# Last products of each row tile half by half of the width, and retention's output projection begun ahead of the last head's turn

## The chip, the cores and the metric

The kernel runs on one core of one Trainium2 chip. TensorE multiplies, VectorE and ScalarE split the weights and do the elementwise work, GpSimd does powers of small columns, SyncE issues the weight loads. The metric is the device time of one launch in microseconds; the kernel before has a median of 3464.42 us over three runs (3463.05 to 3464.59).

## The reference

Two blocks run one behind the other on 256 rows of width 1024, all in float32. Cut to what matters here:

```
# first block, two layers
for l in range(2):
    x = x + 0.5 * swiglu(rms_norm(x, g), w_gate_up, w_down)          # f10, f11
    u = rms_norm(x, mix_norm) @ w_in
    y = concat([ssd_mixer(u), mlstm_mixer(u), rwkv7_mixer(u)])       # m0, m1
    x = x + y @ w_out                                                # out0, out1
    x = x + 0.5 * swiglu(rms_norm(x, g), w_gate_up, w_down)          # f20, f21
x = rms_norm(x, final_norm)
# second block, two layers, x beside a context of 256 rows until the second mixer
half_ffn(t, m, j) = t + 0.5 * m[3j+2] * swiglu_2(modulate(rmsnorm(t), m[3j], m[3j+1]))
layer 0: x, ctx = half_ffn(.,0)  [half00]; += m[5] * fourier_layer  [four]; half_ffn(.,2)  [half02]
layer 1: x, ctx = half_ffn(.,0)  [half10]; x += m[5] * retention    [ret, retout]; x = half_ffn(x,2)  [half12]
return rmsnorm(x, final_g)
# retention, per head: two-sided decayed attention y; then
out = (silu(g) * (y - mean) * rsqrt(var + eps)) @ ret_w_out          # 2048 x 1024
```

## The kernel before, in words

Every large product is done in three passes on split numbers: a float32 matrix is written as a high and a low part, and `mm3` (L103, each product at L100) issues high by high, high by low and low by high into one PSUM bank. A weight tile is [128, 2048] elements (1 MB). SyncE loads it into one of up to eight `raw` places; ScalarE writes its high part into one of two or three `hi` buffers (`split_hi`, L305); VectorE writes the low part over the raw place (`split_lo`, L311). Half-width or single-chunk tiles have 1024 columns.

The program is a list of stages, each a set of generators, one for each engine, that are stepped together: `run(stage)` in `network` appends one phase of a stage to an order, and every engine issues its own instructions of each phase in that order. `Core.plan` attaches the weight tiles to phases and puts each `split_hi`/`split_lo` at the earliest phase at which its `hi` buffer is free and no more than the allowed number of tiles is ahead. Each instruction counts up a semaphore; other engines wait on the count (`mark`, `wait_ge`). Each engine executes in order.

A stage's output projection: the K rows of the product come in chunks of 128, two chunks to a weight tile. The result rows come in tiles `t` of 128 (two for 256 rows, four with the context), the 1024 columns in two halves `h` of 512, and each (t, h) has its own PSUM bank. For all groups of tiles but the last the order is chunk, then row tile, then half. The last group (two weight tiles together, in Fourier one) goes row tile by row tile: for each `t` all its chunks, and inside each chunk both halves. When the last product of (t, h) is done, its bank is marked `back`, and VectorE drains it into the residual: `Half` (L717) and `Whole` (L2438) in one operation, `Gated` in two (L699 multiplies by the gate, L701 adds). The next stage's `Norm` squares each half row on ScalarE as it is finished, takes the power on GpSimd, scales (L588 on VectorE, ScalarE beside it), and TensorE transposes the normed rows (L546) for the next products. `join` interleaves the last phases of a stage with the first of the norm.

High buffers (`his`): 3 for the feed-forward stages of 256 rows (f10, f20, f11, f21, half12), 2 for those of 512 rows (half00, half02, half10), for the mixers' projections (`MixOut`: out0, out1) and for retention's (`Out`). The feed-forward stages have 22 chunks (the 512-row ones in two parts of 11, whose last tile holds a single chunk); `MixOut` and `Out` have 16 chunks, tiles 0 to 7, and the last group is tiles 6 and 7.

Retention (`Ret`) has 26 phases: for each of four heads the projections of q, k, v and gate, the scores, the product with v, silu of the gate (ScalarE, L2826), the normed and gated `y` (VectorE, L2876), eight transposes of it (L2787, the "turn") into banks 4 and 5, and two copies into `yT` (ScalarE, L2831). Then `Out` waits for all of `Ret` (`enter`), splits `yT` in four quarters into `ys` high (L2407) and low (L2416), and runs its products into banks 4 to 7. `ys` lies over the normed rows that `Ret` reads. The gate vector of the residual is made by the `Gates` stage in bank 3, four transposing products at a time (L100 on `retdg`), stepped between the first phases of `Out`.

Of the kernel before, what the change touches and what calls it, by code (L numbers as in the profile page):

```python
# [729 lines left out]
class Ffn(Stage):  # L730
# [44 lines left out]
    def tensor(self, p):  # L775
# [3 lines left out]
        for k, count in enumerate(self.parts):  # L779
            K.ada_bank = 3 if nt == 2 else 7 - 4 * (k % 2)  # L780
            K.ada_bank_free = self.dv["out", k - 1, 3, 1] if k else None
            for j in range(count):
                wh, wl = (w.rearrange("p (k h n) -> p k h n", k=8, h=2) for w in self.ready(p, n))
                if nt == 2 and J >= 3:
                    p.wait_ge(*self.dv["mul", J - 3])
                if nt == 4 and j >= 2:
                    p.wait_ge(*self.dv["mul", J - 2])
                elif nt == 4 and k:
                    p.wait_ge(*self.dv["out", k - 1, j, 1])
                for h, o in enumerate(self.pair(k, J)):  # L790
                    for c in range(8):
                        if J == 0:
                            self.norm.ready(p, c)
                        x = mm3(p, o, wh[:, c, h, :], wl[:, c, h, :], hs[0][:, c, 0:N], hs[1][:, c, 0:N], c == 0, c == 7)
                x.then_inc(*p.mark(self.pe, "tile", n))
                n, J = n + 1, J + 1
                yield
            if nt == 4:
                K.ada.clear(p)
            if self.finish.gates:  # L800
                self.finish.gates.done(p)
            if nt == 4 and k:
                p.wait_ge(*self.dv["out", k - 1, 3, 1])
            for group in self.groups[k]:
                parts = [(i, c) for i in group for c in range(min(2, count - 2 * i))]
                ends = group == self.groups[k][-1]
                if ends:
                    order = [(a, t) for t in range(nt) for a in parts]
                else:
                    order = [(a, t) for a in parts for t in range(nt)]  # L810
                for at, ((i, chunk), t) in enumerate(order):
                    wh, wl = (w.rearrange("p (c n) -> p c n", n=1024)[:, chunk, :] for w in self.ready(p, n + i - group[0]))
                    j = 2 * i + chunk
                    p.wait_ge(*self.dv["lo", J - count + j])
                    if j == 0 and nt == 4 and t >= 2:
                        p.wait_ge(*self.dv["mul", J + t - 4])
                    rows = slice(t * 128, (t + 1) * 128)
                    for h in range(2):
                        c = slice(h * 512, (h + 1) * 512)
                        x = mm3(p, self.back(k, t, h)[:, :], hf[0][:, j, rows], hf[1][:, j, rows], wh[:, c], wl[:, c],  # L820
                                j == 0, j == count - 1)
                        if at == len(order) - 1 and h == 1:
                            x.then_inc(*p.mark(self.pe, "tile", n + len(group) - 1))
                        elif j == count - 1:
                            x.then_inc(*p.mark(self.pe, "back", k, t, h))
                    if ends and (i, chunk) == parts[-1] and t < nt - 1:
                        yield
                n += len(group)
                yield
# [1456 lines left out]
class MixOut(Stage):  # L2286
# [25 lines left out]
    def tensor(self, p):  # L2312
# [2 lines left out]
        p.wait_ge(*self.ssd.dv["lo", 7])  # L2315
        for q in range(7):
            parts = [(q + i, c) for i in range(2 if q == 6 else 1) for c in range(2)]
            order = [(a, t) for t in range(2) for a in parts] if q == 6 else [(a, t) for a in parts for t in range(2)]
            for at, ((n, c), t) in enumerate(order):
# [3 lines left out]
                for h in range(2):  # L2323
# [6 lines left out]
                if q == 6 and t == 0 and last:  # L2330
                    yield
            yield

# [29 lines left out]
class Out(Stage):  # L2363
# [3 lines left out]

    his, phases, tail = 2, 9, 2

    def __init__(self, K, who, after, src, yT, ys, finish, places):  # L2370
        super().__init__(K, "out", who, after)
        self.places = places
        self.yT, self.ys, self.finish = yT, ys, finish
        tiles = back_tiles(src, 0, 16)
        for q in range(7):
            self.tiles[q + 1] = tiles[q:q + 1] if q < 6 else tiles[6:8]
        self.last_of[6] = 7

    def tensor(self, p):
        K, ys = self.K, self.ys  # L2380
        self.enter(p)
        yield
        for q in range(7):
            parts = [(q + i, c) for i in range(2 if q == 6 else 1) for c in range(2)]
            order = [(a, t) for t in range(2) for a in parts] if q == 6 else [(a, t) for a in parts for t in range(2)]
            for at, ((n, chunk), t) in enumerate(order):
# [4 lines left out]
                for h in range(2):  # L2391
# [7 lines left out]
                if q == 6 and t == 0 and (n, chunk) == parts[-1]:  # L2399
                    yield  # L2400
            yield

    def scalar(self, a):
        self.enter(a)
        for i in range(4):
            s = slice(4 * i, 4 * i + 4)
            a().activation(self.ys[0][:, s, :], self.yT[:, s, :], ACT.Copy).then_inc(*a.mark(self.ac, "ys", i))  # L2407
        for _ in range(9):
            yield

    def vector(self, v):
        self.enter(v)
        for i in range(4):
            s = slice(4 * i, 4 * i + 4)
            v.wait_ge(*self.ac["ys", i])
            v().tensor_tensor(self.ys[1][:, s, :], self.yT[:, s, :], self.ys[0][:, s, :].bitcast(F32),  # L2416
                              ALU.subtract).then_inc(*v.mark(self.dv, "ys", i))
# [21 lines left out]
class Fourier(Stage):  # L2439
# [37 lines left out]
    def tensor(self, p):  # L2477
# [38 lines left out]
        self.finish.gates.done(p)  # L2516
        for q in range(4):
            wh, wl = (w.rearrange("p (c n) -> p c n", n=1024) for w in self.ready(p, q))
            order = [(jj, t) for jj in range(2) for t in range(4)] if q < 3 else [(jj, t) for t in range(4) for jj in range(2)]
            for at, (jj, t) in enumerate(order):  # L2520
                j, c = 2 * q + jj, slice(t * 128, (t + 1) * 128)
                for h in range(2):
# [4 lines left out]
                    if at == 7 and h == 1:  # L2527
# [3 lines left out]
                if q == 3 and jj and t < 3:  # L2531
                    yield
            yield

# [151 lines left out]
class Ret(Stage):  # L2686
# [7 lines left out]
    def __init__(self, K, who, norm, yT, ct, m):  # L2694
# [54 lines left out]
    def tensor(self, p):  # L2749
# [4 lines left out]
        for h in range(4):  # L2754
# [37 lines left out]
    def scalar(self, a):  # L2792
# [11 lines left out]
        for h in range(4):  # L2804
# [23 lines left out]
            yield  # L2828
            for q in range(2):
                a.wait_ge(*E["turn", h, q])  # L2830
                a().activation(self.yT[:, 4 * h + 2 * q:4 * h + 2 * q + 2, :], v256(ps[4 + q]),  # L2831
                               ACT.Copy).then_inc(*a.mark(A, "yT", h, q))
            yield

# [59 lines left out]
def network(K):  # L2894
# [219 lines left out]
    rout = put("retout", Out(K, "retout", [ret], A["ret_w_out_2"][0], yT, ys, Gated(gates, K.xa, rot), 6))  # L3114
# [180 lines left out]
```

## Time and profile before

| what | value |
|---|---|
| median of three runs | 3464.42 us (3463.05 to 3464.59) |
| the profiled execution | 3463.73 us, span 3461.7 us |
| mean granted TensorE clock | 0.972 |
| TensorE busy | 3247.6 us, 94% |
| VectorE busy | 2101.1 us, 61% |
| ScalarE busy | 1308.7 us, 38% |

Times in the views are microseconds from the span's start. A row of the timeline gives start, duration, engine, line, operation and the tiles written and read; the brackets give the idle time of that engine before it and what ended it. A matmul's duration is its latency, and successive matmuls overlap, so their rate is read from the differences of their starts.

### The profile page before, as it was taken

Reading aid. Unit: us, or ns where it says so; the run is one execution under the profiler, and the core shown is the slowest. Engines: PE = TensorE matmul, PEld = TensorE weight load, DVE = VectorE, ACT = ScalarE, POOL = GpSimd, SP = SyncE. Lnnn points to the kernel's source line nnn. Section 1 sums busy time; section 2 is a strip of 40 time slices with the busy share of each in tenths; the row PEclk is TensorE's granted clock in tenths of the full one; section 3 lists DMA queues with packets and bytes.
Section 4 is the critical chain, followed back from the end, with each engine's and each line's share of the span. In section 5 each row is a group of like instructions: output and inputs, shape, how many; then the busy total and the mean of one; then the engine's idle time right before and its main releaser. Section 6 shows DMA issues by size and latency. Waiting matters only on the chain.

```text
span 3461.7 us, 45970 instructions
## 1 busy us (share of the span) xinstructions
PE 3247.6 (94%) x19010; PEld 2824.2 (82%) x19010; DVE 2101.1 (61%) x2545; ACT 1308.7 (38%) x1584; POOL 115.8 (3%) x126
## 2 busy tenths in 40 slices
PE   7998988999998898899999999999999999999998
PEld 7978877898988786798788877788878888787797
DVE  6757557776866657677775754775343333544654
ACT  4434244444435234543421233422233122444443
POOL 0001200000000210000000000000000000000000
PEclk9999999999999998999999999999999999999999
DMA  6542022555553112455443531343222222323452
GB/s 250 230 152 86 27 95 77 200 235 204 211 207 104 38 60 72 177 208 211 153 164 123 183 124 37 122 165 122 91 85 98 91 98 80 118 98 109 164 183 98
DMA packets 83835, 462.96 MB, mean 134 GB/s; under 512 B 7573, under 2 KB 11285, under 8 KB 43562
## 3 DMA queue, kind: packets, MB, share of 16 engines
q1 hardware_dynamic: 77952, 451.45, 35.6%
q10 hardware_dynamic: 5674, 8.57, 0.8%
q8 instruction: 150, 2.46, 0.3%
q14 instruction: 59, 0.48, 0.0%
HBM read 458.95 MB, written 1.05 MB: 133 GB/s over the span
## 4 chain that ended last, share of the span: by engine, by line
PE 64%; DVE 25%; ACT 7%; issue 2%; DMA 0%; ACTq 0%; POOL 0%; DVEq 0%; POOLq 0%
PE ps L100 64%; DVE lo L311 8%; DVE acc L459 5%; ACT hi L305 3%; PE ps L546 1%; DVE acc L456 0%; DVE m0restMs L1980 0%; DVEq L86 0%; DVE xt L701 0%; DVE f11rot L875 0%; DVE f10rot L875 0%; DVE f20rot L875 0%; ACT f20hf_h L853 0%; ACT f11hf_h L853 0%; ACT f10hf_h L853 0%
## 5 line engine op out<-in xcount | busy, mean ns | idle before, releaser
L311 DVE TENSOR_TENSOR lo<-raw,hi 128x2048 fp32r<-128x2048 f32 (+1 forms) x357 | 809.6, 2268 | 622.8 <-ACT hi L305 601.5
L305 ACT ACTIVATE hi<-raw 128x2048 fp32r<-128x2048 f32 (+1 forms) x357 | 676.1, 1894 | 572.7 <-PE ps L100 541.9
L459 DVE SCALAR_TENSOR_TENSOR acc<-raw,sil,acc 128x512 f32<-128x512 f32 x504 | 379.0, 752 | 20.7 <-DVE f21hf_l L877 0.5
L100 PE MATMUL ps<-half00hs,hi 128*128 128x512 f32 x672 | 209.3, 393 | 0.6 <-DVE lo L311 0.6
L100 PE MATMUL ps<-half02hs,hi 128*128 128x512 f32 x672 | 209.0, 392 | 0.7 <-DVE lo L311 0.7
L100 PE MATMUL ps<-half10hs,hi 128*128 128x512 f32 x672 | 208.7, 392 | 0.8 <-DVE lo L311 0.7
L100 PEld LDWEIGHTS ps<-half10hs,hi 128*128 128x128 f32 x672 | 125.7, 188 | 28.5 <-DVE lo L311 1.6
L100 PEld LDWEIGHTS ps<-half02hs,hi 128*128 128x128 f32 x672 | 125.4, 188 | 27.6 <-DVE lo L311 1.1
L100 PEld LDWEIGHTS ps<-half00hs,hi 128*128 128x128 f32 x672 | 125.2, 188 | 27.3 <-DVE lo L311 1.0
L100 PE MATMUL ps<-half10hs,lo 128*128 128x512 f32 x352 | 137.6, 391 | 0.0
L100 PE MATMUL ps<-half02hs,lo 128*128 128x512 f32 x352 | 137.6, 391 | 0.0
L100 PE MATMUL ps<-half00hs,lo 128*128 128x512 f32 x352 | 137.6, 391 | 0.0
L100 PE MATMUL ps<-half12hs,hi 128*128 128x256 f32 x704 | 127.9, 285 | 0.5 <-DVE half12hs L625 0.5
L100 PE MATMUL ps<-hi,half00hf 128*128 128x512 f32 x352 | 109.7, 391 | 2.1 <-DVE mods L469 1.4
L100 PEld LDWEIGHTS ps<-half12hs,hi 128*128 128x128 f32 x704 | 109.8, 192 | 1.1 <-DVE half12hs L625 0.9
L100 PE MATMUL ps<-hi,half02hf 128*128 128x512 f32 x352 | 109.6, 391 | 0.5 <-DVE lo L311 0.5
L100 PE MATMUL ps<-hi,half10hf 128*128 128x512 f32 x352 | 109.3, 390 | 0.0
L100 PE MATMUL ps<-f10hs_h,hi 128*128 128x256 f32 x352 | 101.1, 287 | 7.6 <-DVE lo L311 6.9
L100 PE MATMUL ps<-f20hs_h,hi 128*128 128x256 f32 x352 | 100.8, 286 | 4.1 <-DVE lo L311 3.3
L100 PE MATMUL ps<-f21hs_h,hi 128*128 128x256 f32 x352 | 102.6, 291 | 2.0 <-DVE lo L311 1.1
L100 PE MATMUL ps<-f11hs_h,hi 128*128 128x256 f32 x352 | 100.9, 287 | 2.3 <-DVE lo L311 1.7
L100 PE MATMUL ps<-f21hs_l,hi 128*128 128x256 f32 x352 | 101.3, 288 | 0.0
(919 smaller groups left out, 7900.3 us busy)
## 6 DMA issues: line engine op xcount, KB each, us to landing
raw<-in_ffn_w_gate_up SPq DMA_DIRECT2D x88, 1024.0 KB, 9.0
raw<-in_ffn_gu SPq DMA_DIRECT2D x88, 1024.0 KB, 5.0
raw<-in_ffn_w_down SPq DMA_DIRECT2D x85, 1024.0 KB, 5.2
raw<-in_ada_w SPq DMA_DIRECT2D x72, 1024.0 KB, 5.1
raw<-in_w_in_t SPq DMA_DIRECT2D x28, 1024.0 KB, 5.0
raw<-in_ret_w_in SPq DMA_DIRECT2D x24, 1024.0 KB, 4.9
raw<-in_w_out SPq DMA_DIRECT2D x16, 1024.0 KB, 5.0
raw<-in_w_in_n SPq DMA_DIRECT2D x12, 1024.0 KB, 5.0
```

The lines of the kernel that those rows point to most:

```text
L100: return p().matmul(o, l, r, start=start, stop=stop, skip_group_check=True)
L305: a().activation(self.high(w), self.raw[self.place(r)][:, 0:width], ACT.Copy).then_inc(*a.mark(self.wac, w))
L311: v().tensor_tensor(self.low(w), self.raw[self.place(r)][:, 0:width], self.high(w).bitcast(F32), ALU.subtract).then_inc(*v.mark(self.wdv, w))
L459: v().scalar_tensor_tensor(out=acc[:, n, :], in0=w[:, k, :], scalar=s, in1=acc[:, n, :], op0=ALU.mult, op1=ALU.add).then_inc(*v.mark(self. ...
L546: x = p().transpose(b[:, t * 128:(t + 1) * 128], self.xs[:, 2 * s + t, c * 128:(c + 1) * 128], K.ident)
```

## The change

It has two parts.

1. In the last group of `Ffn`, `MixOut`, `Out` and `Fourier` the order becomes row tile, then half, then chunk: all chunks of (t, 0), then all chunks of (t, 1). The products are the same, and so are the marks on them.
2. `Out` no longer waits for the whole of `Ret`. Its ScalarE part waits for the last product of `Ret` that reads the normed rows (tile 23), its first products wait for the banks that `Ret` used (`emptied`), and each quarter of `ys` is split in its own place in the order: quarter 0 in the first phase, 1 and 2 in the second, 3 in the third. The order of phases becomes `Out`, `Ret`, `Out`, `Ret`, `Out`, gates, `Out`, gates, `Out`, gates, where `Ret`'s two are its last: the multiplication by the gate on VectorE, and the turn. The last head's turn goes to banks 0 and 1.

```
 Ffn.tensor
                 if ends:
-                    order = [(a, t) for t in range(nt) for a in parts]
+                    order = [(a, t, [h]) for t in range(nt) for h in range(2) for a in parts]
                 else:
-                    order = [(a, t) for a in parts for t in range(nt)]
+                    order = [(a, t, range(2)) for a in parts for t in range(nt)]
...
-                    for h in range(2):
+                    for h in hs2:
...
-                    if ends and (i, chunk) == parts[-1] and t < nt - 1:
+                    if ends and (i, chunk) == parts[-1] and h == 1 and t < nt - 1:
                         yield
 MixOut.tensor and Out.tensor
-            order = [(a, t) for t in range(2) for a in parts] if q == 6 else [(a, t) for a in parts for t in range(2)]
+            order = ([(a, t, [h]) for t in range(2) for h in range(2) for a in parts] if q == 6 else
+                     [(a, t, range(2)) for a in parts for t in range(2)])
 Fourier.tensor
-            order = [(jj, t) for jj in range(2) for t in range(4)] if q < 3 else [(jj, t) for t in range(4) for jj in range(2)]
+            order = ([(jj, t, range(2)) for jj in range(2) for t in range(4)] if q < 3 else
+                     [(jj, t, [h]) for t in range(4) for h in range(2) for jj in range(2)])
 Out
+    def emptied(self, p, t, h):
+        p.wait_ge(*(self.ret.ac["g", 3, 0] if (t, h) == (1, 1) else self.ret.dv["y", 3, 1]))
     def tensor(self, p):
-        self.enter(p)
         yield
...
+                    if (q, chunk) == (0, 0):
+                        self.emptied(p, t, h)
     def scalar(self, a):
-        self.enter(a)
+        a.wait_ge(*self.ret.pe["tile", 23])
         for i in range(4):
             s = slice(4 * i, 4 * i + 4)
             a().activation(self.ys[0][:, s, :], self.yT[:, s, :], ACT.Copy).then_inc(*a.mark(self.ac, "ys", i))
-        for _ in range(9):
-            yield
+            if i != 1:
+                yield
+        for _ in range(6):
+            yield
+    def head(self, v, i):
+        s = slice(4 * i, 4 * i + 4)
+        v.wait_ge(*self.ac["ys", i])
+        v().tensor_tensor(self.ys[1][:, s, :], self.yT[:, s, :], self.ys[0][:, s, :].bitcast(F32),
+                          ALU.subtract).then_inc(*v.mark(self.dv, "ys", i))
     def vector(self, v):
-        self.enter(v)
-        for i in range(4):
-            s = slice(4 * i, 4 * i + 4)
-            v.wait_ge(*self.ac["ys", i])
...
+        self.head(v, 0)
         yield
         for q in range(7):
+            for i in ((1, 2), (3,))[q] if q < 2 else ():
+                self.head(v, i)
 Ret
+    def turned(self, h):
+        return 4 if h < 3 else 0
-                        x = p().transpose(ps[4 + q][:, (2 * m + t) * 128:(2 * m + t + 1) * 128],
+                        x = p().transpose(ps[self.turned(h) + q][:, (2 * m + t) * 128:(2 * m + t + 1) * 128],
 network
-    for _ in range(ret.phases):
+    for _ in range(ret.phases - 2):
         run(ret)
-    for q in range(rout.phases - rout.tail):
+    for s in (rout, ret, rout, ret, rout, gates, rout, gates, rout, gates):
+        run(s)
+    for _ in range(rout.phases - rout.tail - 5):
         run(rout)
-        if q < 3:
-            run(gates)
```

## Rows read from the trace of the kernel before

**Rows 1.** The page, sections 1 and 4: busy time, and the chain that ended last.
```profile
PE 3247.6 (94%) x19010; PEld 2824.2 (82%) x19010; DVE 2101.1 (61%) x2545; ACT 1308.7 (38%) x1584; POOL 115.8 (3%) x126
...
PE 64%; DVE 25%; ACT 7%; issue 2%; DMA 0%; ACTq 0%; POOL 0%; DVEq 0%; POOLq 0%
```

**Rows 2.** Who waited for whom, TensorE: us in total, times, longest us.
```profile
PE ps L100 <- DVE lo L311: 36.9, 35, 3.0
...
PE ps L546 <- DVE half00xs L588: 7.0, 1, 7.0
```

**Rows 3.** Timeline, last group of out0: start us, us, engine line op, [idle before <-releaser].
```profile
609.77 0.39 PE L100 MATMUL ps<-hi,m0ys_h 128*128 128x512 f32 x1
...
610.02 3.92 ACT L305 ACTIVATE hi<-raw 128x2048 fp32r<-128x2048 f32 x2 [4.40 <-PE ps L100]
...
612.27 0.39 PE L100 MATMUL ps<-hi,m0ys_l 128*128 128x512 f32 x1
614.32 0.50 PE L100 MATMUL ps<-hi,m0ys_h 128*128 128x512 f32 x1 [1.67 <-DVE lo L311]
```

**Rows 4.** Timeline, last two drains of f10 (VectorE, two merged).
```profile
224.78 1.49 DVE L717 SCALAR_TENSOR_TENSOR xt<-ps,xt 128x512 f32<-128x512 f32 x2 [2.93 <-PE ps L100]
```

**Rows 5.** Timeline, VectorE, last group of half02.
```profile
2545.95 1.22 DVE L311 TENSOR_TENSOR lo<-raw,hi 128x1024 fp32r<-128x1024 f32 x1 [7.94 <-ACT hi L305]
...
2560.51 0.69 DVE L699 TENSOR_TENSOR half02fin<-ps,half02gb 128x512 f32<-128x512 f32 x1 [0.23 <-PE ps L100]
...
2562.03 0.69 DVE L699 TENSOR_TENSOR half02fin<-ps,half02gb 128x512 f32<-128x512 f32 x1
```

**Rows 6.** TensorE after two idle pieces (timeline), then granted clock (PEclk) in four stretches (windows).
```profile
247.75 0.58 PE L100 MATMUL ps<-m0hx_h,hi 128*128 128x256 f32 x1 [2.97 <-DVE lo L311]
...
1061.45 0.39 PE L100 MATMUL ps<-m1hx_h,hi 128*128 128x256 f32 x1 [2.88 <-DVE lo L311]
...
core 0: us, PE busy (x) PEld busy (x) DVE busy (x) ACT busy (x) POOL busy (x), PEclk, DMA share, GB/s
246.80:253.60 6.80, 5.85 (x27) 5.85 (x28) 4.15 (x4) 1.65 (x1) 0.00 (x0) 0.50 0.30 125
1062.50:1065.90 3.40, 3.40 (x19) 3.40 (x18) 2.29 (x1) 0.00 (x0) 0.00 (x0) 0.51 0.06 24
615.40:618.80 3.40, 3.40 (x16) 2.79 (x15) 2.65 (x3) 1.22 (x3) 0.00 (x0) 1.00 0.61 251
3199.30:3209.50 10.20, 6.98 (x21) 5.49 (x19) 6.39 (x9) 7.33 (x7) 0.00 (x0) 0.50 0.14 58
```

**Rows 7.** Timeline, last group of f21: low half of its second tile, and the product on it.
```profile
1648.55 2.29 DVE L311 TENSOR_TENSOR lo<-raw,hi 128x2048 fp32r<-128x2048 f32 x1
...
1650.89 0.50 PE L100 MATMUL ps<-hi,f21hf_h 128*128 128x512 f32 x1
```

**Rows 8.** Timeline, VectorE, the last drain of the Fourier stage.
```profile
2169.03 0.69 DVE L699 TENSOR_TENSOR four_fin<-ps,four_gb 128x512 f32<-128x512 f32 x1 [0.39 <-PE ps L100]
```

**Rows 9.** Timeline, VectorE, second drain of half12's first row tile.
```profile
3448.28 0.69 DVE L699 TENSOR_TENSOR half12fin<-ps,half12gb 128x512 f32<-128x512 f32 x1
```

**Rows 10.** Timeline, retention's last head to its projection; first the turn of head 0.
```profile
3030.94 1.03 PE L2787 MATMUL ps<-msk,ct 128*128 128x128 f32 x8
...
3196.63 1.23 ACT L2826 ACTIVATE rg<-ps 128x512 f32<-128x512 f32 x2
...
3198.98 1.72 PE L2787 MATMUL ps<-msk,ct 128*128 128x128 f32 x8 [2.55 <-DVE ct L2876]
...
3201.36 3.23 ACT L2407 ACTIVATE ys_h<-retyT 128x1024 fp32r<-128x1024 f32 x3
...
3202.55 2.56 DVE L2416 TENSOR_TENSOR ys_l<-retyT,ys_h 128x1024 fp32r<-128x1024 f32 x2 [3.62 <-ACT ys_h L2407]
...
3203.92 0.77 PE L100 MATMUL ps<-hi,ys_h 128*128 128x512 f32 x1 [3.22 <-DVE ys_l L2416]
...
3212.11 1.05 PE L100 MATMUL ps<-retdg,msk 128*128 128x128 f32 x8
```

More of the change, by code:

```diff
@@ L807, in tensor @@
                 if ends:
-                    order = [(a, t) for t in range(nt) for a in parts]
+                    order = [(a, t, [h]) for t in range(nt) for h in range(2) for a in parts]
                 else:
-                    order = [(a, t) for a in parts for t in range(nt)]
-                for at, ((i, chunk), t) in enumerate(order):
+                    order = [(a, t, range(2)) for a in parts for t in range(nt)]
+                for at, ((i, chunk), t, hs2) in enumerate(order):
                     wh, wl = (w.rearrange("p (c n) -> p c n", n=1024)[:, chunk, :] for w in self.ready(p, n + i - group[0]))
@@ L2317, in tensor @@
             parts = [(q + i, c) for i in range(2 if q == 6 else 1) for c in range(2)]
-            order = [(a, t) for t in range(2) for a in parts] if q == 6 else [(a, t) for a in parts for t in range(2)]
-            for at, ((n, c), t) in enumerate(order):
+            order = ([(a, t, [h]) for t in range(2) for h in range(2) for a in parts] if q == 6 else
+                     [(a, t, range(2)) for a in parts for t in range(2)])
+            for at, ((n, c), t, hs) in enumerate(order):
                 wh, wl = (w.rearrange("p (c n) -> p c n", n=1024)[:, c, :] for w in self.ready(p, n))
@@ L2322, in tensor @@
                 first, last, rows = (n, c) == (0, 0), (n, c) == (7, 1), slice(t * 128, (t + 1) * 128)
-                for h in range(2):
+                for h in hs:
                     s = slice(h * 512, (h + 1) * 512)
@@ L2329, in tensor @@
                         x.then_inc(*p.mark(self.pe, "back", t, h))
-                if q == 6 and t == 0 and last:
+                if q == 6 and t == 0 and h == 1 and last:
                     yield
@@ L2368, with __init__ @@
     his, phases, tail = 2, 9, 2
-    def __init__(self, K, who, after, src, yT, ys, finish, places):
-        super().__init__(K, "out", who, after)
-        self.places = places
+    def __init__(self, K, who, ret, src, yT, ys, finish, places):
+        super().__init__(K, "out", who)
+        self.places, self.ret = places, ret
         self.yT, self.ys, self.finish = yT, ys, finish
@@ L2384, in tensor @@
             parts = [(q + i, c) for i in range(2 if q == 6 else 1) for c in range(2)]
-            order = [(a, t) for t in range(2) for a in parts] if q == 6 else [(a, t) for a in parts for t in range(2)]
-            for at, ((n, chunk), t) in enumerate(order):
+            order = ([(a, t, [h]) for t in range(2) for h in range(2) for a in parts] if q == 6 else
+                     [(a, t, range(2)) for a in parts for t in range(2)])
+            for at, ((n, chunk), t, hs) in enumerate(order):
                 wh, wl = (w.rearrange("p (c n) -> p c n", n=1024)[:, chunk, :] for w in self.ready(p, n))
@@ L2390, in tensor @@
                 rows = slice(t * 128, (t + 1) * 128)
-                for h in range(2):
+                for h in hs:
                     c = slice(h * 512, (h + 1) * 512)
+                    if (q, chunk) == (0, 0):
+                        self.emptied(p, t, h)
                     x = mm3(p, K.ps[4 + 2 * t + h][:, :], ys[0][:, j, rows], ys[1][:, j, rows], wh[:, c], wl[:, c],
@@ L2398, in tensor @@
                         x.then_inc(*p.mark(self.pe, "back", t, h))
-                if q == 6 and t == 0 and (n, chunk) == parts[-1]:
+                if q == 6 and t == 0 and h == 1 and (n, chunk) == parts[-1]:
                     yield
@@ L2518, in tensor @@
             wh, wl = (w.rearrange("p (c n) -> p c n", n=1024) for w in self.ready(p, q))
-            order = [(jj, t) for jj in range(2) for t in range(4)] if q < 3 else [(jj, t) for t in range(4) for jj in range(2)]
-            for at, (jj, t) in enumerate(order):
+            order = ([(jj, t, range(2)) for jj in range(2) for t in range(4)] if q < 3 else
+                     [(jj, t, [h]) for t in range(4) for h in range(2) for jj in range(2)])
+            for at, (jj, t, hs) in enumerate(order):
                 j, c = 2 * q + jj, slice(t * 128, (t + 1) * 128)
-                for h in range(2):
+                for h in hs:
                     b, ns = K.ps[2 * t + h], slice(h * 512, (h + 1) * 512)
@@ L2526, in tensor @@
                         x = mm3(p, b[:, :], *(f[0:5, c] for f in self.fx), *(w[0:5, ns] for w in self.wxs), False, True)
-                    if at == 7 and h == 1:
+                    if at == len(order) - 1 and h == 1:
                         x.then_inc(*p.mark(E, "tile", q))
@@ L2530, in tensor @@
                         x.then_inc(*p.mark(E, "back", t, h))
-                if q == 3 and jj and t < 3:
+                if q == 3 and jj and h == 1 and t < 3:
                     yield
@@ L2830, in scalar @@
                 a.wait_ge(*E["turn", h, q])
-                a().activation(self.yT[:, 4 * h + 2 * q:4 * h + 2 * q + 2, :], v256(ps[4 + q]),
+                a().activation(self.yT[:, 4 * h + 2 * q:4 * h + 2 * q + 2, :], v256(ps[self.turned(h) + q]),
                                ACT.Copy).then_inc(*a.mark(A, "yT", h, q))
@@ L3113, in network @@
     gates = put("retgates", Gates(K, "retg", [ret], 1, 1, 1, 1.0, gb, dg, 3))
[L3114 removed]
+    rout = put("retout", Out(K, "retout", ret, A["ret_w_out_2"][0], yT, ys, Gated(gates, K.xa, rot), 6))
     join(half, norm)
[L3116 removed]
+    for _ in range(ret.phases - 2):
         run(ret)
[L3118 removed]
+    for s in (rout, ret, rout, ret, rout, gates, rout, gates, rout, gates):
+        run(s)
+    for _ in range(rout.phases - rout.tail - 5):
         run(rout)
[L3120 to L3121 removed]
     norm, gates, half = half_ffn(1, 2, 2, [22], K.xa, rout, 8192, 16384, (53248, 61440), 69632, 79872, 75776, (8192, 30720),
```

2 lines of the change are left out of this document (removed).

## The prediction, made before the changed kernel was run

> **What bounds the kernel.** I read the page first: TensorE is busy 94% of the span, and of the chain that ended last 64% is its own products, 25% VectorE [rows 1]. So TensorE sets the time wherever it isn't kept waiting, and the change adds and removes no large product: it reorders. The second view is who waited for whom, TensorE alone: the largest entry is the low half of a weight tile, 36.9 us in 35 waits; a wait for the normed rows after a residual update is at most 7.0 us [rows 2]. The third is the timeline around each place where the diff acts: twelve tails (the last group of products of a stage) and the passage from retention to its output projection. At a tail two things matter: when VectorE can drain the last bank, and when the second weight tile of the group must be ready. The profiled execution took 3463.73 us (span 3461.7 and 2.0 around it), 0.7 under the median of the runs, 3464.42; the sum is made against it and 0.7 is added.
>
> **The unit.** In a last group before the change each chunk of 128 rows serves both halves of the width; a chunk and a half are three products. Twelve starts from 609.77 to 612.27 are 0.227 us apart [rows 3], so one half of a chunk is 0.68 us, and two chunks of one half are 1.36 us.
>
> **Tails with two high-half buffers: both mixer outputs and retention's projection.** The second tile of the group (number 7) can be split only when tile 5 is released: ScalarE starts on it at 610.02, and TensorE, released by VectorE's low half, resumes at 614.32 after 1.67 us idle [rows 3]. The same stands twice more, at 1430.38 (1.66) and 3245.82 (1.67). Before the change twelve products (two chunks, both halves) cover part of that split; after it only six do, since the first half now wants all four chunks before the second half begins. TensorE resumes at the same moment with six more products to do: +1.36 us each, and the stall grows from 1.67 to 3.03. Given back: VectorE's last drain no longer queues behind the drain of the other half. In a plain residual update this queue is small: two drains take 1.49 us, the second product chain ends 0.68 after the first, so 0.12 is gained [rows 4]; in a gated one each half is two operations, 1.52 us from drain to drain (2560.51 to 2562.03) [rows 5], so 0.84 is gained. Net: mixer outputs +1.24 twice, retention's projection +0.52; together +3.0.
>
> **The clock at these three.** After 2.97 us idle the products from 247.75 ran beside a granted clock of 0.50 until 253.6; after 2.88 us idle, from 1062.5 to 1065.9 at 0.51; after the 1.67 us stall the clock stayed at 1.00 [rows 6]. (2.4 GHz against 1.2.) So I expect that a stall of 3.03 brings what 2.9 brought. The products here are dense, so half a stretch at the low level is lost: 1.7 us for the short stretch, up to 2.9 for the long one, nothing if the clock holds. I take 1.7 each, the stretch at 1062.5, since in it too the products run without gaps: +5.1 (bounds 0 and 8.7). The Trainium skill (TensorE: Matmul & The Clock Gate, "HAM oscillation") warns that a kernel which waits between bursts pays the slow start again after each wait, but only for gaps longer than this one. By that rule the sum would be 5.1 lower; the 2.88 us gap in this trace speaks against it.
>
> **The first-block FFN tails f10, f20, f11.** They have three high-half buffers; with the third the second tile is split one group earlier, so nothing new waits. Gain 0.12 each [rows 4]: -0.4. The tail of f21 differs: the split of the second tile is late, ending at 1650.84, and TensorE's product starts at 1650.89 [rows 7]; it had waited 0.1. Six products fewer before it: +1.36, less 0.12: +1.24. The stall of 1.5 us is below the 1.67 that left the clock alone.
>
> **Four-row FFN tails (half00, half02, half10).** The last tile holds one chunk. In half02 its low half ends at 2547.17; the group's 72 products of 0.23 us end near 2561.2, so it starts near 2544.7, and before the change it was in time for the thirteenth product, about 2547.5; now the seventh wants it at 2546.1. TensorE resumes at 2547.2 with six more to do: its end moves by 1.1 to 1.2. Against it stands the drain queue: the last row's drains start at 2560.51 and 2562.03 though its second half could be ready at 2561.19, 0.84 earlier [rows 5]. Net +0.3 each, +0.9 for three. The first groups of these stages end in a single chunk: order unchanged, 0.
>
> **Fourier.** One tile of two chunks, no second tile to wait for. The last drain starts at 2169.03 after 0.39 us idle, released by TensorE [rows 8]: no queue, so 0.
>
> **The last FFN (half12) and the end of the kernel.** Three high buffers, tiles in time. VectorE's second drain of row tile 0 starts at 3448.28 with no idle before it, queued behind the first like that of half02, 0.84 after its products could be ready [rows 9]; everything behind it (squares, scale, then row tile 1's two drains at 0.10 us distance) is one chain to the end. -0.84.
>
> **Retention to its projection.** Before: the last products of the heads end at 3196.43; silu of the gate until 3197.86, multiplication, eight transposes from 3198.98 after 2.55 idle (1.72 us at the low clock), two copies, split of ys, first product at 3203.92 after 3.22 idle; its 24 products and the next piece of work are apart by 8.19 us instead of 5.44 because the clock was 0.50 until 3209.5 [rows 6, 10]. After: the first product needs only the first quarter of ys. ScalarE is in order: silu until 3197.86, then 1.08 for ys high (3.23 for three), to 3198.95; VectorE then 1.23 plus the handover, to 3200.25; first product at 3200.3. The banks are free (the y copies are read before the squares that precede the silu, the gate's first bank by 3197.3). The idle is then one piece of 3.9, again followed by the low clock; I charge 2.3 against the 2.75 of before (bounds 0 and 3.4). So the first tile ends at 3200.3+5.44+2.3 = 3208.0, and the transposes follow: 1.03 for eight at full clock as at 3030.94, some 0.8 of it not overlapped: 3208.8. Before, this point was 3212.11 [rows 10]: -3.3. On the path behind it: VectorE must do the multiplication (1.6), the split of tile 1 (2.3) and two quarters of ys (2.6) behind the first quarter, from 3200.3 to about 3206.8, under cover of the first tile; tile 2's high half waits on ScalarE behind the two copies of the turn and its low half is ready some 5.1 us after the turn, with 5.4 us of products to cover it. If that cover of 0.3 is gone the loss is some tenths, for which I keep 0.2. Banks 0 and 1 for the last turn cost nothing: their last reader, the product with the decay, is ahead of the y copies. I take -3.1 (bounds -1.0 and -5.4). SyncE's tile queue sees the releases of the same tiles in the same order; no transfer is late, as no wait of these rows ends on one.
>
> **Sum.** +3.0 +5.1 -0.4 +1.24 +0.9 +0 -0.84 -3.1 = +5.9. 3463.73 + 5.9 + 0.7 = 3470.3 us.
>
> **Rivals.** (A) The clock holds through the three longer stalls. For it: a gap in which the low level starts depends on what ran before; against it: both gaps near 3 us that I quote. Then +0.8: 3465.2. (B) The low level lasts as long as from 247.75 at each of the three stalls: 2.9 instead of 1.7, +9.5: 3473.9, and some of the bounds of retention with it. (C) The other side, faster: the second tile's split isn't what TensorE stands on, so that six fewer products in front of it cost nothing (the high half would have to be made earlier than the release of tile 5). Then the drains' gains alone are left: mixers -0.24, projection and end -1.68, f stages -0.5, four-row tails -2.3, retention -3.1: -7.8, 3456.6. It decides wherever the split ends before the seventh product. Against it: the ScalarE split in rows 3 is itself released by TensorE after 4.40 us idle. (D) Retention's new order stalls on its second or third tile or keeps the low clock for longer: -3.1 becomes -1.0; with the rest as forecast 3472.4.
>
> **Chances.** Forecast 0.50, A 0.16, B 0.17, C 0.07, D 0.10. What a measurement of this kernel can tell from no change is about 0.2%, 6.9 us: 3457.5 to 3471.3. The forecast lies 1.0 under that edge, so I give a third of its chance to slower; with B and D that is 0.44; same 0.49; faster 0.07, C alone. The range reaches from A's side, 3463.5, to B's, 3474.5.
>
> **What would show it.** TensorE idle about 3.0 us before tile 7 in the three projections, and a granted clock of 0.5 behind it; 1.5 us before f21's second tile and about 1.1 in the four-row tails; the wait for the normed rows 0.1 shorter in the plain tails; the last drain of half12 0.8 earlier relative to its products; one idle of 3.9 us before retention's projection, eight transposes at full clock behind 24 products and no wait for the first turn. Unchanged stalls at tile 7 would make the prediction wrong, and so would a long stall at tile 1 or 2 of the projection.

## The result and the profile after

The changed kernel takes 3469.99 us (median of 20 runs, 3465.27 to 3472.4); the kernel before, run between them on the same chip, takes 3461.48 (20 runs, 3458.14 to 3468.62). The ratio is 1.002, 95% interval 1.0014 to 1.0027: slower by 4.8 to 9.3 us. A second job gave 3468.75 against 3462.39, 1.0017 [1.0008, 1.0026]. Forecast: 3470.3, and +5.9 for the difference. The kernel before ran 2.9 below the three runs that the forecast started from, so of the two numbers the difference is the one to judge by. Measured it is 6.9 us by the ratio of 1.002, 8.5 between the two medians and 7.2 between the two means: a little above the forecast, which lies inside the interval. That the absolute time agrees within 0.3 us is luck.

The profiled execution of the changed kernel took 3465.54 us, only 1.8 more than that of before, 3463.73. The page and the waits of TensorE (us in total, times, longest) answer to [rows 1, 2]:

```profile
PE 3241.8 (94%) x19010; PEld 2820.4 (81%) x19010; DVE 2101.5 (61%) x2545; ACT 1308.7 (38%) x1584; POOL 115.9 (3%) x126
...
PE 65%; DVE 24%; ACT 7%; issue 2%; DMA 0%; ACTq 0%; DVEq 0%; POOL 0%; POOLq 0%
```
```profile
PE ps L100 <- DVE lo L311: 44.1, 41, 3.1
...
PE ps L546 <- DVE half12xs L588: 3.7, 1, 3.7
```

The products are the same in number; the wait for a low half has grown from 36.9 to 44.1 us, in 41 waits instead of 35. Where it grew, the timeline shows. At the output of mixer 0 (answers to [rows 3]), at the projection of retention, at f21 [rows 7] and in half00 (in half02 at 2551.97 the wait is 1.07 too):

```profile
609.64 3.92 ACT L305 ACTIVATE hi<-raw 128x2048 fp32r<-128x2048 f32 x2 [4.42 <-PE ps L100]
...
610.53 0.39 PE L100 MATMUL ps<-hi,m0ys_l 128*128 128x512 f32 x1
613.94 0.50 PE L100 MATMUL ps<-hi,m0ys_h 128*128 128x512 f32 x1 [3.02 <-DVE lo L311]
...
1653.95 0.51 PE L100 MATMUL ps<-hi,f21hf_h 128*128 128x512 f32 x1 [1.18 <-DVE lo L311]
...
2054.97 0.50 PE L100 MATMUL ps<-hi,half00hf 128*128 128x512 f32 x1 [1.07 <-DVE lo L311]
...
3247.95 0.50 PE L100 MATMUL ps<-hi,ys_h 128*128 128x512 f32 x1 [3.02 <-DVE lo L311]
```

The split of the second tile starts 4.3 us before TensorE resumes, as before (610.02 to 614.32 then); six products fewer stand in front of it. The granted clock (PEclk) in the stretches behind the three long stalls and at the start of retention's projection:

```profile
core 0: us, PE busy (x) PEld busy (x) DVE busy (x) ACT busy (x) POOL busy (x), PEclk, DMA share, GB/s
615.00:618.40 3.40, 3.40 (x10) 2.66 (x9) 1.97 (x2) 0.72 (x2) 0.00 (x0) 0.50 0.68 277
1430.80:1434.20 3.40, 3.40 (x9) 2.64 (x8) 2.01 (x2) 0.72 (x2) 0.00 (x0) 0.50 0.65 267
3248.00:3251.40 3.40, 3.40 (x15) 2.83 (x16) 3.23 (x3) 0.00 (x0) 0.00 (x0) 1.00 0.00 0
3205.70:3209.10 3.40, 3.06 (x7) 2.49 (x8) 3.06 (x4) 3.11 (x3) 0.00 (x0) 0.50 0.19 76
```

Behind the first stall ten products in 3.4 us where 16 ran in the same time before [rows 6]. From retention to its projection (answers to [rows 10]; ScalarE, VectorE, TensorE):

```profile
3202.37 1.23 ACT L2844 ACTIVATE rg<-ps 128x512 f32<-128x512 f32 x2
3203.63 1.06 ACT L2414 ACTIVATE ys_h<-retyT 128x1024 fp32r<-128x1024 f32 x1
...
3204.72 1.22 DVE L2424 TENSOR_TENSOR ys_l<-retyT,ys_h 128x1024 fp32r<-128x1024 f32 x1 [4.76 <-ACT ys_h L2414]
...
3206.04 0.77 PE L100 MATMUL ps<-hi,ys_h 128*128 128x512 f32 x1 [3.87 <-issue]
3213.07 1.03 PE L2805 MATMUL ps<-msk,ct 128*128 128x128 f32 x8
```

Instead of idle pieces of 2.55 and 3.22 with the turn between them there is one of 3.87, silu, quarter high, quarter low and product are one chain, and the eight transposes run at full clock behind 24 products. The label "issue" means only that the profile names no releaser; the product starts 0.10 after the low quarter ends. At the end of the kernel the second half's drain is no longer queued (answers to [rows 9]); it waits for its products:

```profile
3447.31 0.69 DVE L699 TENSOR_TENSOR half12fin<-ps,half12gb 128x512 f32<-128x512 f32 x1 [3.90 <-PE ps L100]
...
3450.08 0.69 DVE L699 TENSOR_TENSOR half12fin<-ps,half12gb 128x512 f32<-128x512 f32 x1 [1.36 <-PE ps L100]
```

**Two ways to weigh a part.** Whole times carry low-clock stretches anywhere in the program. So I also take the way from one fixed product to another around each part, with few such stretches on it. For a mixer output: from its first product to the first transpose on the next normed rows; in the changed kernel

```profile
597.51 0.48 PE L100 MATMUL ps<-hi,m0ys_h 128*128 128x512 f32 x1
...
628.35 1.93 PE L546 MATMUL ps<-msk,f20xs 128*128 128x128 f32 x9 [2.98 <-DVE f20xs L588]
```

30.84 us, where before it was 28.03 (597.89 to 625.92): 2.81 more, and 2.6 if the way is taken to a product of the next stage, as it is for the table. The way of half00 ends at Fourier's first product, those of the other feed-forward stages and of retention at the next first transpose. By parts, beside the forecast, for the two profiles of the changed kernel:

| part | forecast, us | first | second |
|---|---|---|---|
| two mixer outputs, with clock | +5.9 | +5.2 | +5.1 |
| f10, f20, f11 | -0.4 | -0.4 | -0.4 |
| f21 | +1.24 | +0.93 | +1.04 |
| half00 | +0.3 | +0.74 | +0.74 |
| half02, half10 | +0.6 | +1.0 | +1.0 |
| retention's end to half12's normed rows, with clock | -0.9 | -3.1 | -0.6 |
| end | -0.84 | -0.81 | -0.79 |
| sum | +5.9 | +3.6 | +6.1 |

The first profile as a whole is only 1.8 us longer than that of before, because the pieces between the parts differ as well, with low-clock stretches that stand in one trace and not in the other: -2.6 from the parts at mixer output 0 to output 1, +1.4 in f21's first products, +1.6 ahead of half00's tail, -1.8 in Fourier. At least the last has no cause in the change: in before's trace a low stretch stands at 2158.22, and two kernels whose Fourier stage is as before (mixer outputs alone, again; mixer outputs filled) lack it as well and are 1.5 us shorter there.

### The profile page after: what moved, and what is told of

Same layout as the page of the kernel before. It is cut to its first block, busy times and chain, and to the rows that moved or that the text cites. A ratio compares the mean times of both kernels' runs of the same rounds, so it can differ in the third digit from the quotient of the medians.

```text
span 3463.5 us, 45970 instructions
## 1 busy us (share of the span) xinstructions
PE 3241.8 (94%) x19010; PEld 2820.4 (81%) x19010; DVE 2101.5 (61%) x2545; ACT 1308.7 (38%) x1584; POOL 115.9 (3%) x126
## 4 chain that ended last, share of the span: by engine, by line
PE 65%; DVE 24%; ACT 7%; issue 2%; DMA 0%; ACTq 0%; DVEq 0%; POOL 0%; POOLq 0%
PE ps L100 64%; DVE lo L311 8%; DVE acc L459 5%; ACT hi L305 3%; PE ps L546 1%; DVE acc L456 0%; DVE m1restMs L1980 0%; DVE m0restMs L1980 0%; DVEq L86 0%; DVE f11rot L875 0%; DVE f10rot L875 0%; DVE f20rot L875 0%; ACT f11hf_h L853 0%; ACT f10hf_h L853 0%; ACT f20hf_h L853 0%
```

## The experiments

Each ran in the same job as runs of the kernel before. "Way" is as above.

**Retention's part alone** (all tails as before the change).

```
 # in MixOut, Out, Ffn and Fourier alike:
-order = [(a, t, [h]) for t in range(2) for h in range(2) for a in parts]
+order = [(a, t, range(2)) for t in range(2) for a in parts]
...
```

> Only the retention part of the change; all tails in the order of before. My theory: the first product of the projection comes after one idle of 3.9 us instead of two of 2.5 and 3.2 around the turn, and nothing else moves: 3.1 us faster than before, ratio 0.9991 (0.9984 to 0.9997). Rival (the new order of retention is what costs): slower than before by up to 7 us, ratio up to 1.002. In the trace my theory wants stalls of 1.67 us at tile 7 of all three projections, as before.

3459.11 us against 3460.89, 0.9996 [0.9987, 1.0005]. First product after one idle piece of 3.87, 3.6 us earlier than before; tile 7 waits 1.66 as before. From retention's rows to half12's the way is 2.4 shorter. The trace shows the gain; the whole times can't tell it from nothing.

**The tails alone** (retention and `Out`'s start as before).

```
-for s in (rout, ret, rout, ret, rout, gates, rout, gates, rout, gates):
+for _ in range(ret.phases):
...
 # and Out.tensor, scalar, vector and the place of the turn as before
```

> Only the half-by-half order in the last groups; retention as before. My theory: 3.0 for the three projections net of the shorter drains, 5.1 for the clock behind their longer stalls, +1.2 at f21, +0.9 at the four-row tails, -0.4 and -0.84 at the plain tails and the end: +9 us, ratio 1.0026 (1.0015 to 1.0035). Rival (retention is what costs): about 2 us or less, ratio under 1.0006. A third theory, that products of one bank in a row go slower: the product rate in the last groups changes from 0.227 us; mine says it stays.

3471.37, 1.003 [1.0018, 1.0042]: the loss is the tails'. Three stalls of 3.02, a clock of 0.50 behind each:

```profile
617.10:620.50 3.40, 3.40 (x10) 2.63 (x9) 2.35 (x2) 0.72 (x2) 0.00 (x0) 0.50 0.78 318
1432.90:1436.30 3.40, 3.40 (x9) 2.65 (x9) 1.83 (x2) 0.72 (x2) 0.00 (x0) 0.50 0.60 246
3252.20:3255.60 3.40, 3.40 (x9) 2.63 (x10) 2.87 (x2) 0.00 (x0) 0.00 (x0) 0.50 0.00 0
```

The third theory is out: the last 24 products of f10's stage start 0.227 us apart in this kernel as before, those of half10's 0.231.

**The mixer outputs alone, and with the stall filled.** The second kernel issues twelve more products, whose result nobody reads, into a free bank ahead of tile 7.

```
 # both: MixOut.tensor half by half, all else as before; the second also:
+if (n, c, t) == (7, 0, 0) and 0 in hs:
+    for _ in range(12):
+        mm(p, K.ps[7][:, :], kept[0][:, 0:128], kept[1][:, 0:512])
```

> Only the two mixer outputs go half by half, everything else as before. My theory: stalls at tile 7 of 3.03 instead of 1.67 us, +1.24 each net, and 1.7 to 2.9 each where the clock falls behind it: +5.9 us (2.5 if it falls at neither), ratio 1.0017. Rival (the stall is not TensorE's bound, other work hides it): 0.

> As e3, with twelve idle products (2.7 us, result not used, bank 7) issued by TensorE ahead of its wait for tile 7, so that the stall is filled with activity but the wait ends at the same moment. If the clock behind the stall costs, as I say: the clock stays at 1.0 there, and only +1.24 twice is left against before: +2.5 us, ratio 1.0007, 3.4 less than e3. If the stall alone costs: same as e3.

3468.08, 1.0016 [1.0008, 1.0025], and with the filler 3467.5, 1.0021 [1.0012, 1.003]. In the filled one

```profile
611.23 2.88 PE L100 MATMUL ps<-hi,m0ys_h 128*128 128x512 f32 x12
614.41 0.50 PE L100 MATMUL ps<-hi,m0ys_h 128*128 128x512 f32 x1 [0.30 <-DVE lo L311]
```
```profile
615.30:618.70 3.40, 3.40 (x17) 2.79 (x16) 2.14 (x2) 0.72 (x2) 0.00 (x0) 1.00 0.70 284
1431.00:1434.40 3.40, 3.40 (x17) 2.78 (x16) 2.10 (x2) 0.72 (x2) 0.00 (x0) 1.00 0.72 299
```

the clock holds and the way is 1.21 us over before instead of 2.85: the first is the later resumption (forecast 1.24), the rest, 1.6, the clock (forecast 1.7). A second low stretch, at the transposes behind the output (625.7 before), is gone too, so that at the next stage's products the way is 0.76 over before instead of 2.56. But the filled kernel is no faster in whole. That contradicts the simple reading, so the pair was run again below.

**One tile split between the tail's two orders.** The changed kernel, but in `MixOut` and `Out` tile 6 is used chunk by chunk for both row tiles first, and only tile 7 half by half.

```
-order = [(a, t, [h]) for t in range(2) for h in range(2) for a in parts]
+order = ([(a, t, range(2)) for a in parts[:2] for t in range(2)] +
+         [(a, t, [h]) for t in range(2) for h in range(2) for a in parts[2:]])
```

> The changed kernel, with the last groups of the mixer outputs and of retention's projection reordered again: tile 6 first for both row tiles and both halves (24 products, 5.4 us, which cover the split of tile 7), then tile 7 half by half. My theory (the wait for tile 7 is what costs): no stall at tile 7; against the kernel before 0.12+1.67 gained in each mixer output, about 1.0 in the projection (its first row tile ends later, which gives 1.4 back), and the clock has nothing to fall behind. With retention -3.1, end -0.84, f21 +1.24, four-row tails +0.9 and plain tails -0.4: -5.8 us, ratio 0.9983; 12 us under the changed kernel. Rival (order itself or luck of the clock costs): no difference from the changed kernel, 1.002.

3459.44 against 3461.73, 0.9995 [0.9986, 1.0004]: some 9 us under the changed kernel (each by its own runs of before, as they come from two jobs), where 12 were forecast; against before it can't be told from nothing. TensorE's waits:

```profile
PE ps L100 <- DVE lo L311: 35.6, 37, 2.9
...
PE ps L546 <- DVE half12xs L588: 5.2, 1, 5.2
```

24 products instead of six now stand between the release of tile 5's buffer and tile 7, and no stall is left there. A part comes back: with less work behind the first row tile's last drain, the normed rows of half12 are waited for 5.2 us, not 3.7 (4.5 before).

**Half by half in the last row tile only.** Where only the last row tile is drained late, the first can keep the old order, whose twelve products cover the split. Half12 stays half by half in both.

```
-order = [(a, t, [h]) for t in range(nt) for h in range(2) for a in parts]
+order = [(a, t, hh) for t in range(nt) for hh in
+         ([[0], [1]] if t == nt - 1 or half12 else [range(2)]) for a in parts]
```

> The changed kernel, but half by half only in the last row tile of each last group (in the last feed-forward stage in both); the other row tiles take both halves of each chunk as before. My theory: the second tile is wanted after twelve products again, stalls 1.67 at tile 7, 0.1 at f21, none in the four-row tails; the drains' gains stay: mixers -0.24, projection -0.84, plain tails -0.5, four-row tails -0.7, end -0.84, retention -3.1: -6.2 us, ratio 0.9982. Rival: 1.002 as the changed kernel.

3458.06, 0.9986 [0.9977, 0.9995]. Tile 7 waits 1.66 and 1.67, f21 and the four-row stages lose nothing more. What the change loses is gone, and most of what it gains is kept. Of the 0.7 us forecast for the last drains of the four-row stages there are 0.3: 0.12 and 0.19 in half02 and half10, none in half00.

**The best of each.** Retention's start as changed; `MixOut` and `Out` with tile 7 alone half by half; f21 and the four-row stages half by half in the last row only; f10, f20, f11, Fourier and half12 as changed.

```
+whole = nt == 2 and self.key != "f21"
+order = [(a, t, hh) for t in range(nt) for hh in
+         ([[0], [1]] if t == nt - 1 or whole else [range(2)]) for a in parts]
```

> The pieces that I expect to gain, together: retention's new start; mixer outputs and projection as in e5 (no stall at tile 7); f21 and the four-row tails half by half in the last row tile only; the other feed-forward tails and the Fourier tail as in the changed kernel. By my terms: -3.1 -3.6 -1.0 -0.5 -0.7 -0.84 = -9.7 us, ratio 0.9972 (0.996 to 0.9985). Rival (these terms are swamped by where the low clock falls): within 0.0015 of 1.

3453.32 (3451.94 to 3455.91), 0.9975 [0.9966, 0.9983]: faster than both kernels, by 5.9 to 11.8 us than before (forecast 9.7). The waits for low halves fall under before's 36.9 [rows 2]:

```profile
PE ps L100 <- DVE lo L311: 30.3, 32, 2.2
```

**The changed kernel with its three stalls filled.**

```
 # MixOut as above, and in Out:
+if (n, chunk, t) == (7, 0, 0) and 0 in hs:
+    for _ in range(12):
+        mm(p, K.ps[3][:, :], ys[0][:, 13, 0:128], kept[:, 0:512])
```

> The changed kernel, with twelve idle products (result not used) ahead of the wait for tile 7 in both mixer outputs and in retention's projection. In e4 the trace showed the clock at 1.0 behind the filled stalls and a step of +1.3 where e3 had more, yet over the runs e4 was no faster than e3. If the low clock behind these three stalls costs on average: 3 to 5 us under the changed kernel, ratio 1.0006 to 1.001. If on average it does not, or the filling costs as much elsewhere, as e4's runs say: 1.002, as the changed kernel.

3467.86, 1.0014 [1.0005, 1.0023]. Again a little, not the 5.1 us that the clock was charged with.

**The two pairs again, in one job.**

> The changed kernel once more, in one job with its filled form and with the two kernels that change the mixer outputs alone. Open is whether the low clock behind a stall of 3.02 us recurs from execution to execution. Theory (the clock follows the gap): tile 7 of both mixer outputs waits 3.0 us, the granted clock behind it is 0.5 for 3.4 us again, and from the output's first product to the first transpose of the next rows it takes 2.8 us more than before, as in the first profile (of which 1.2 is the later resumption). Rival (where the low clock falls is chance of the execution): one or both of the two stretches are absent, and the way is 1.2 longer where they are. Median about 3469 in either case, 1.002 of before.

> The changed kernel with twelve idle products ahead of tile 7 in the three projections, in the same job as the changed kernel. Theory: no low clock behind tile 7; the way from each mixer output's first product to the next transposes is 1.2 us over before instead of 2.8, so 3.2 us less than the changed kernel for the two and up to 4.8 with the projection: 3465 beside 3469. Rival: the low clock that is kept away here falls elsewhere, and the medians agree within 1.5 us.

> Half by half in the two mixer outputs alone. Theory: +2.6 us each over before, 5.2 in all, so 1.0015 of before; 0.5 clock behind both stalls. Rival: +1.2 each with stretches that come and go, 1.0007.

> The same with twelve idle products ahead of tile 7. Theory: +0.75 each, 1.5 in all, 1.0004 of before, 3.7 us under the kernel without them. Rival: no difference to it, as the first pair of runs had it (1.0021 beside 1.0016).

Changed kernel 3468.75 and filled 3468.03 (1.0017 and 1.002 of before); mixer outputs alone 3467.52 and filled 3465.75 (1.0017 and 1.0015). In the traces the stretches recur where the first profiles had them. The changed kernel, then the filled one, behind the three places of tile 7:

```profile
615.60:619.00 3.40, 3.40 (x10) 2.62 (x9) 1.95 (x2) 0.72 (x2) 0.00 (x0) 0.50 0.64 263
1431.40:1434.80 3.40, 3.40 (x9) 2.64 (x8) 2.01 (x2) 0.72 (x2) 0.00 (x0) 0.50 0.62 255
3250.70:3254.10 3.40, 3.40 (x9) 2.61 (x9) 2.92 (x3) 0.00 (x0) 0.00 (x0) 0.50 0.00 0
```
```profile
615.90:619.30 3.40, 3.40 (x16) 2.77 (x16) 2.28 (x2) 0.72 (x2) 0.00 (x0) 1.00 0.72 296
1431.50:1434.90 3.40, 3.40 (x16) 2.78 (x16) 2.28 (x2) 0.72 (x2) 0.00 (x0) 1.00 0.72 301
3244.00:3247.40 3.40, 3.10 (x14) 2.24 (x13) 3.30 (x2) 1.14 (x1) 0.00 (x0) 1.00 0.37 154
```

Over all unfilled profiles 12 of 13 stalls of 3.02 us have a clock of 0.5 behind them (the exception stands in the first profile after, at 3248); of 10 filled ones none has, and of the 13 stalls of 1.66 or 1.67 us in all traces none has. So locally the theory holds, in the one profiled execution of each kernel that can be looked into; chance of the execution doesn't explain the stretches. In the whole time the rival holds: the two jobs together give means of 3468.97 (30 runs) and 3467.55 (22) for the changed kernel without and with filler, 1.4 apart, and 3467.65 and 3467.09 (22 each) for the mixer outputs alone, 0.6 apart, each difference uncertain by some 1.4 (the kernel before has medians of 3461.48, 3461.73 and 3462.39 in the jobs that are put together here). Two stretches were worth 3.2 to 3.7 on the way. The granted clock, which is on record for each execution, says the same: its mean goes from 0.9737 to 0.9744 with the filler (changed kernel) and from 0.9728 to 0.9733 (mixer outputs), each uncertain by 0.0006; a stretch of 3.4 us at half the clock is 0.0005 of a span of 3465, so 0.0015 and 0.0010 were due. By these means about half of the low clock that is kept away there stands elsewhere, with room from little to nearly all of it.

One place can be named. From mixer output 0's first product to output 1's the four unfilled profiles take 815.8 to 815.9 us and the four filled ones 815.6 to 815.8 (before 816.05), though at the next stage's first products they were 1.8 apart: before the second output begins, the first one's saving is gone. Low stretches at the first transposes behind f20, which the filled traces have (as before) and the unfilled ones lack, are one part of it. From output 1's first product to half00's transposes the filled traces stay 3 us shorter; where that is paid for in the timed executions, no trace shows.

The other kernels lean the same way. Sum of the parts in the trace against the timed difference to before (the ratio less 1, times before's median), us:

| kernel | sum of parts | timed |
|---|---|---|
| changed, and again | +3.6, +6.1 | +6.9, +5.9 |
| tails alone | +7.6 | +10.4 |
| mixer outputs alone, and again | +5.1, +5.0 | +5.5, +5.9 |
| retention alone | -2.8 | -1.4 |
| mixer outputs filled, and again | +1.5, +1.5 | +7.3, +5.2 |
| changed and filled, and again | +0.6, -0.4 | +4.8, +6.9 |
| tile 7 alone half by half | -7.3 | -1.7 |
| last row only | -6.5 | -4.8 |
| best | -11.8 | -8.6 |

Timed differences are uncertain by about 3. Where the mixers keep a stall, parts and time agree within 3.3; where it is filled or gone, the time is 3.2 to 7.3 us worse than the parts. The single differences are hardly beyond their uncertainty, and all but one of the smaller ones lie on that side too; that the larger ones are all six of those without a stall is what speaks.

## Why the prediction was right, step by step

**Nearly all stalls were right to hundredths.** Tile 7: forecast 3.03, measured 3.02, three times, released by VectorE's low half that ends no earlier. Four-row stages: 1.1 forecast, 1.07 measured. f21: 1.5 forecast, 1.18 measured; what shortened it by 0.3 I didn't trace, but in the five profiles of kernels that leave f21's order alone (retention alone, the mixer outputs alone and filled) its way is 0.07 to 0.29 shorter than in before's trace as well. Rival C (six fewer products cost nothing) is out by the same rows. That these stalls cost time is shown by the kernels that take them away: with tile 7's stall gone some 9 us less than the changed kernel, with the last row only some 12 less (from two jobs, each against its own runs of before).

**The drains.** -0.12 each in f10, f20, f11: measured -0.11 to -0.14 from the last product to the transposes. The end: -0.84 forecast, -0.81 measured; the kernels with the old order in half12's stage (mixers alone) show 0.

**The four-row stages were mis-sized, half00 by 0.4 and the others by 0.2.** I took TensorE's delay to be the 1.1 to 1.2 us of its idle time. It is 1.33 or 1.34 in all three: from the first to the last product of the group 16.42 us (2046.45 to 2062.87) became 17.76 (2052.34 to 2070.10) in half00. Behind the idle piece the first product's start is 1.46 us and the second's 0.34 us after the one ahead, where 0.23 is the rule, so the idle time alone is too little. With the drain's 0.84 this gives +0.50, as measured in half02 (+0.49) and half10 (+0.51). In half00 the first transposes don't wait for the last drain; two later ones do, for VectorE's L701. Before, then after the change:

```profile
2063.11 1.14 PE L2492 MATMUL ps<-msk,fxs 128*128 128x128 f32 x9
...
2065.98 0.44 PE L2492 MATMUL ps<-msk,fxs 128*128 128x128 f32 x2 [1.40 <-DVE ct L701]
```
```profile
2070.34 0.93 PE L2505 MATMUL ps<-msk,fxs 128*128 128x128 f32 x7
...
2072.37 0.44 PE L2505 MATMUL ps<-msk,fxs 128*128 128x128 f32 x2 [0.56 <-DVE ct L701]
```

So the first transposes come 1.34 later, the wait for the drain is 0.84 shorter as forecast, and the next wait, for ScalarE's copy, takes 0.25 of that back (0.94 before, 1.19 after): +0.74 at Fourier's first product. With the last row tile alone in the new order the wait is 1.41, and nothing is gained.

**Retention.** In its own count the first product was to start at 3200.3; it starts at 3206.04 in a trace in which everything since retention's first rows is 5.75 late, that is at 3200.29. The idle piece is 3.87 for 3.9. Of the size (-3.1 by the turn's end, bounds -1.0 and -5.4) the kernel with this part alone shows -2.4 on the way through the projection. With the projection's tail (+0.52) and 1.7 for the clock the forecast is -0.9; measured -3.1 in the first profile and -0.6 in the second. The first has no low stretch behind tile 7 and 3.4 us of low clock at retention's start; the second has one of 3.4 behind tile 7 and 6.8 at the start (before: 10.2). The cover of 0.3 behind the turn held: no wait shows up at tiles 1 and 2. Rival D is out.

**The clock is the open term.** That the gap of 3.0 brings the low level, and at 1.6 us a time on the way (forecast 1.7), is shown: 12 of 13 with it, none of 10 without. By the rule of the Trainium skill cited ahead (TensorE: Matmul & The Clock Gate, "HAM oscillation": only longer gaps pay again) none of the three should have; the traces disagree with that. But +5.1 as a net term of the whole time is not shown: filling the gap gives back 1.4 (changed kernel) and 0.6 (mixers), each uncertain by 1.4, not 5.1 and 3.4. So Rival A (the clock at no net cost) is nearer for this term in size, and wrong in its reason. That the forecast of the difference is near the measurement is therefore in part luck: the four-row stages (+0.8 over the forecast), the 0.7 missing in retention and whatever the low level does elsewhere take the place of the rest. The total of low-clock time doesn't settle it: 193.0 us in the profile before, 174.7 and 185.1 in the two after, 186.4 and 167.6 in the two filled. Which mechanism puts low stretches elsewhere when they are kept away in one place, the runs don't show.

## What to carry to other kernels

Before reordering the products on a pair of tiles, count how many of them stand between the release of the buffer and the first use of the second tile: here that count, times 0.227 us, gave all three stalls at tile 7 with 12, with 6 and (none) with 24 products. A stall costs a little more than its idle time (1.34 us for 1.07 here). Take the finer order only where a drain at the end is waited for, which is the last row tile, and keep the coarse order in front of the tile that comes late; the gain was then had without the loss (0.9975). What a shorter queue of drains is worth is read from the next stage's waits, all of them and not the first alone: half00's first transposes didn't wait for the last drain, two later ones did.

## What was not expected of the hardware

- Keeping the clock up in one place didn't shorten the program: a way of 31 us became 1.6 us shorter, in four of four filled profiles at each mixer output, and the program of 3465 us by 0.6 and 1.4, each uncertain by 1.4.
- Executions of one kernel in one job differ by up to 11 us (3456.91 to 3467.82 for the kernel before), and the time goes with the mean granted clock, 0.971 to 0.977: over all runs about 1.5 us for 0.001, with 1.5 us left unexplained. Differences of 2 us between two profiles of such a kernel are of that kind; only ways between fixed instructions could be compared to a tenth.
- Twelve products of no use, 2.88 us, did not delay TensorE: it resumed at the low half's end as without them (the way is 1.19 to 1.23 us over before in all filled profiles, 1.24 by the count of products and drains).
